# Two small columns, a table and small statistics move behind the work area, and every moving piece of a split product begins at 256 modulo 512 bytes

## The reference

```
u = rms_norm(x, g_mix[l]) * (1 + sc_a) + sh_a
proj = u @ w_in[l]
...
x = x + gt_a * (merged @ w_out[l])
u = rms_norm(x, g_ffn[l]) * (1 + sc_f) + sh_f
h = jax.nn.silu(u @ w_ffn_gate[l]) * (u @ w_ffn_up[l])
x = x + gt_f * (h @ w_ffn_down[l])
```

## Time and profile before

| | us |
|---|---|
| median of three runs | 2111.57 (2110.25 to 2115.39) |
| the profiled execution's own time | 2112.94 |
| its span, first to last instruction | 2111.1 |
| TensorE busy | 2038.4 (97%) |
| VectorE busy | 1624.9 (77%) |
| ScalarE busy | 1172.6 (56%) |
| mean granted TensorE clock | 0.992 |

### The profile page before, as it was taken

The page is one execution under the profiler, slowest core; times in us unless marked ns, Lnnn a source line. Parts: engine busy times, 40 slices in busy tenths (PEclk is TensorE's granted clock), DMA queues, the critical chain, the costliest instruction groups (busy, mean ns, idle before and its releaser), DMA issues.

```text
span 2111.1 us, 37052 instructions
## 1 busy us (share of the span) xinstructions
PE 2038.4 (97%) x13975; PEld 1849.3 (88%) x13975; DVE 1624.9 (77%) x2668; ACT 1172.6 (56%) x2116; POOL 148.0 (7%) x233
## 2 busy tenths in 40 slices
PE   6999999999999999998999999999999999999998
PEld 6988989999988989998876888888888888999997
DVE  7888879966688879978788789786889426657984
ACT  6757756645557756645637555352544226656762
POOL 0100000000000000004000210101102000000000
PEclk9999999999999999999999999999999999999999
DMA  9756547865666557876441334546644232243553
GB/s 359 277 205 207 173 159 249 277 233 167 224 231 208 171 170 236 293 250 199 153 165 48 124 120 150 192 148 224 222 143 140 90 100 91 91 151 132 187 183 117
DMA packets 106624, 383.03 MB, mean 181 GB/s; under 512 B 11504, under 2 KB 16128, under 8 KB 105184
## 3 DMA queue, kind: packets, MB, share of 16 engines
q1 hardware_dynamic: 77584, 280.21, 39.2%
q0 software_dynamic: 25792, 94.31, 13.5%
q10 hardware_dynamic: 3088, 6.29, 0.8%
HBM read 379.71 MB, written 1.05 MB: 180 GB/s over the span
## 4 chain that ended last, share of the span: by engine, by line
PE 80%; DVE 10%; DMA 3%; issue 3%; ACT 3%; POOL 0%; POOLq 0%; SPq 0%; DVEq 0%; ACTq 0%
PE ps L1100 20%; PE ps L1103 19%; PE ps L1104 19%; PE ps L1121 3%; PE ps L1125 3%; PE ps L1126 3%; DVE ring_l L2380 2%; DVE ada_junk L2403 2%; DMA work<-adas_in 2%; PE ps L1143 2%; PE ps L1147 1%; PE ps L1146 1%; PE ps L1673 1%; DMA ring<-tape_in 1%; PE ps L1338 1%
## 5 line engine op out<-in xcount | busy, mean ns | idle before, releaser
L1100 PE MATMUL ps<-part,ring_l 128*128 128x256 f32 (+1 forms) x3445 | 1040.9, 302 | 12.5 <-DVE ring_l L2380 8.1
L1103 PE MATMUL ps<-part,ring_r 128*128 128x256 f32 (+1 forms) x3445 | 1032.3, 300 | 0.0
L1104 PE MATMUL ps<-part,ring_r 128*128 128x256 f32 (+1 forms) x3445 | 1029.6, 299 | 0.0
L2380 DVE TENSOR_TENSOR ring_l<-ring,ring_r 128x1024 fp32r<-128x1024 f32 x514 | 626.5, 1232 | 151.0 <-ACT ring_r L1723 148.6
L1723 ACT ACTIVATE ring_r<-ring 128x1024 fp32r<-128x1024 f32 x514 | 533.8, 1056 | 362.9 <-DMA ring<-tape_in 264.9
L1100 PEld LDWEIGHTS ps<-part,ring_l 128*128 128x128 f32 x3445 | 649.3, 188 | 45.9 <-issue 7.6
L1104 PEld LDWEIGHTS ps<-part,ring_r 128*128 128x128 f32 x3445 | 649.4, 189 | 23.8
L1103 PEld LDWEIGHTS ps<-part,ring_r 128*128 128x128 f32 x3445 | 649.6, 189 | 22.1
L2403 DVE SCALAR_TENSOR_TENSOR ada_junk<-work 128x1024 bf16<-128x1024 f32 x272 | 333.9, 1228 | 49.2 <-DMA work<-adas_in 37.4
L1143 PE MATMUL ps<-part,ring_l 128*128 128x256 f32 (+1 forms) x400 | 125.2, 313 | 21.0 <-DVE part L2380 11.5
L1146 PE MATMUL ps<-part,ring_r 128*128 128x256 f32 (+1 forms) x400 | 121.6, 304 | 0.0
(11 more groups left out here) (287 smaller groups left out, 2110.9 us busy)
## 6 DMA issues: line engine op xcount, KB each, us to landing
ring<-tape_in SPq DMA_DIRECT2D x514, 512.0 KB, 3.4
work<-adas_in POOLq DMA_DIRECT2D x176, 512.0 KB, 4.7
work<-ada_first_in SPq DMA_DIRECT2D x8, 1024.0 KB, 17.2
work<-bias_in ACTq DMA_DIRECT2D x1, 2048.0 KB, 8.0
x<-x_t_in SPq DMA_DIRECT2D x1, 1024.0 KB, 7.6
work<-cond_in POOLq DMA_DIRECT2D x1, 1024.0 KB, 8.9
x<-ctx_in ACTq DMA_DIRECT2D x1, 1024.0 KB, 9.8
x<-dist_in ACTq DMA_DIRECT2D x1, 1024.0 KB, 6.1
```

The source lines that it names most:

```text
L1100: mm = pe.matmul(dst, lhsT=wl, rhs=mr, start=(k == 0), stop=False)
L1103: pe.matmul(dst, lhsT=wr, rhs=mr, start=False, stop=False)
L1104: mm = pe.matmul(dst, lhsT=wr, rhs=ml, start=False, stop=(k == len(moving) - 1))
L2380: return dve.tensor_tensor(dst, whole, rounded_part.bitcast(F32), ALU.subtract)
```

## The change

`fill` goes. `gs_mix`, `gs_ffn` and `misc` are laid behind `work`. Together these are 256 bytes, so `work` begins at 103,680, which is 256 modulo 512. The second stack's statistics (`na_max`, `na_sum`, `na_recip`, `ln_sum`, `ln_var`, `ln_rstd`) are laid in the last 108 floats of `work`, so `U2` begins at float 512. No instruction, wait or transfer is added, removed or put in another order. The start of the rings, and with it that of the weights, stays at 128 modulo 512.

```diff
-FILL = 8
...
-        gs_mix = sb("gs_mix", KD)
-        gs_ffn = sb("gs_ffn", KD)
...
-        misc = sb("misc", N_MISC)
...
-        fill = sb("fill", FILL)
...
         with nc.sbuf_tensor("work", [P, WORK + (ADA_SLOTS + N_COND) * D], F32) as work:
-            pass
+            with nc.sbuf_tensor("gs_mix", [P, KD], F32) as gs_mix, nc.sbuf_tensor("gs_ffn", [P, KD], F32) as gs_ffn, \
+                    nc.sbuf_tensor("misc", [P, N_MISC], F32) as misc:
+                pass
...
-        LN = place(3, 4)
-        ln_sum, ln_var, ln_rstd = (at(LN + 4 * n, 4) for n in range(3))
-        na_max, na_sum, na_recip = carve(2 * H, 2), carve(2 * H, 2), carve(2 * H, 2)
+        SMALL = WORK - 108
+        na_max, na_sum, na_recip = (at(SMALL + 4 * H * n, 2 * H, 2) for n in range(3))
+        ln_sum, ln_var, ln_rstd = (at(SMALL + 12 * H + 4 * n, 4) for n in range(3))
...
-        assert taken[0] <= WORK
+        assert taken[0] <= SMALL, taken[0]
```

More of the change, by code:

```diff
@@ L572, in two_blocks @@
         na_probs += [[at(SGU_B, T2), at(NA_BIAS, T2)], [carve(T2), at(NA_BIAS + H * T, T2)]]
-        assert taken[0] <= WORK
+        assert taken[0] <= SMALL, taken[0]
         na_keys = [at(SGU_W, 4, T), at(MIX_T, 4, T)]
         WIDE_SQ, WIDE_Y = BASE2, BASE2 + 12 * D
-        assert WIDE_Y + KD * T2 <= WORK and BASE2 + 9 * D < SGU
+        assert WIDE_Y + KD * T2 <= SMALL and BASE2 + 9 * D < SGU
         taken[0] = BASE2
@@ L591, in two_blocks @@
         wide_h = carve(2, T2)
-        assert taken[0] <= WORK, taken[0]
+        assert taken[0] <= SMALL, taken[0]
         taken[0] = BASE2
```

## The result

The changed kernel takes 2124.71 us (median of four runs, 2123.99 to 2124.97) against 2112.1 before (2110.25 to 2115.39). The ratio is 1.0056 with a 95% interval of 1.0038 to 1.0074: slower by 12.6 us. The forecast was 2071, with 0.20 for slower. What happened is rival 2, forecast at 2126.

The account below looks back on a forecast made before the run. TensorE, busy for 97% of the span, was taken as the bound, its pace hanging on operand starts. Gains of 28.1, 15.1 and 4.0 us, less 4.7 and 2.0, left 40.5 us: 2071 us, range 2038 to 2124.

Parts of the forecast that it names:

- rival 2: Moving pieces' starts: the pattern repeats at 256 bytes or less, so 256 is as 0; slower, 2126 us, chance 0.20.
- The start decides the possible paces and not the pace alone: TensorE's matmuls: products settle in one of several paces; one start, 448, showed both 117.7 and 113.4 ns.
- If closeness below the weights' start is what costs, 256 is among the good starts: Moving pieces: 256 lies furthest from 0, so it was given the trace's shortest step, 113.4 ns.
- The 28.1 us priced for the first stack: Gain for 5307 matmuls of 256 columns starting at 0, from 118.7 to 113.4 ns each.
- the 113.4 ns that I took for a start of 256: Step assumed for 256-column matmuls after the change, taken from the last output products at 448.
- the 15.1 us for the pieces at 448: Gain for 3500 of 4329 matmuls of 256 columns at 448, from 117.7 to 113.4 ns each.
- the 4.0 us for 512 columns: Gain for 1905 matmuls of 512 columns at 448, from 228.9 to 226.8 ns each.
- 10% for the chain's other links: Discount where the chain runs over VectorE, ScalarE or a transfer; 4.7 us off the main forecast's gain.
- The steps at 0 stay at 118.7 through long stretches: 256-column matmuls starting at 0: evidence that their pace differs from that at 448, against the start doing nothing.
- The stream's 233.3 at a start of 128: Streams of 512 columns, moving piece at 128: slower than 228.9 ns at 448, used as support for 256.
- Rival 1: TensorE's matmuls: the start does nothing or has small effects; time 2107 to 2113 us, chance 0.15.
- VectorE as the next limit: First feed-forward: TensorE would need 81.2 us while VectorE has 83.2 us of work, so 2.0 us are lost.

Follow-up runs that it names:

- all_192: Changed kernel with `par1_all` also laid behind `work`, so all moving pieces begin at 192 modulo 512: 2105.71 us, ratio 0.9967.
- all_440: `all_192` with `par` also behind `work` and every view of `work` shifted by 6 floats, so activations begin at 440: 2129.3 us, ratio 1.0086.
- ring192_work256: Changed kernel with 64 bytes ahead of the ring and `par1_all` behind a shorter `work`: weights at 192, activations at 256; 2106.68 us, ratio 0.9972.
- ring_r192_work256: Changed kernel with 64 bytes between the rings and `par1_all` behind a shorter `work`: `ring_l` at 128, `ring_r` at 192, activations at 256; 2101.65 us.
- base_only: Changed kernel with the statistics in front of `U2` again: first stack's gate and up pieces at 256, later ones at 192; 2109.22 us, ratio 0.9985.
- ring_r192_stack2_192: `ring_r192_work256` with the statistics in front again, so pieces from the down products on begin at 192: 2105.41 us, ratio 0.9975.

## Why the prediction was wrong

*What bounds the kernel, and that only addresses matter.* Right. Counts, waits and other engines are as before, and the loss lies in TensorE's steps.

*The start decides the possible paces and not the pace alone.* Right. At a distance of 64 a run of products settles at 113.3 or 117.8 ns; at 0 no 24 steps in a row have a mean below 118.2 ns in any of the three traces with all pieces there, and some run at 120.0. It might also explain why single times of a kernel at 64 scatter from 2098 to 2115 us (`all_192`, ten runs) and those of the changed kernel over 1 us (four runs). That is not shown: no kernel has several traces, and `all_440`, whose trace holds no short step, scatters from 2126 to 2140 us in five runs.

*The step that failed: "If closeness below the weights' start is what costs, 256 is among the good starts".* The idea that what matters lies between the moving piece and the weights beside it was right; `ring192_work256` shows it. I measured that distance around a circle of 512 bytes, for which I had no row. It repeats at 256 bytes, or at a part of that: 0, 128 below the weights' start, and 256, 128 above it, step alike, and so do 448 and 192, both 64 above it modulo 256. On that circle the change moves nothing for the first stack and takes everything else from the best place to one of the poor ones. The 28.1 us priced for the first stack came to nothing, since its step stayed at 118.7; the 113.4 ns that I took for a start of 256 occurs there in no stretch of 24 steps, the shortest of which has 118.2; the 15.1 us for the pieces at 448 had the wrong sign, as had the 4.0 us for 512 columns.

*Rival 2* priced the same facts as 7.7 us for 256 columns and 8.4 for 512. The traces have 6.5 and 8.3. Its one discount, 10% for the chain's other links, was small: 14.8 us became 12.1 in the span, 18% less, and no run shows that those links were the reason. It had 0.20 on the ground that no row told a period of 512 from one of 256 or 128. With two starts seen and the third unknown, that was the even question, and I answered it by the picture that I liked.

*Where rows were misread.* "The steps at 0 stay at 118.7 through long stretches" holds for the rows that I showed; other long stretches at 0 step at 120.0. Of the matmuls at 448 the trace has 725 short steps (at most 114.5 ns) where I took 800, but of the second layer's down products a quarter are short (139 of 581) and not most. The stream's 233.3 at a start of 128 was taken as a hint that a moving piece near the weights' place is slow. In fact streams step at 232 to 234 ns at every uniform distance, so they were no evidence about the activations.

*Rival 1 and the rule behind it.* The Trainium skill (TensorE: Matmul & The Clock Gate, section Step-by-step: what each phase is for) says that loading the next tile's weights takes no read bandwidth from the running matmul. If that were all, the place of the weights could not matter to the step. For float32r at full clock it does: 512-column activations at 256 step at 233.1 ns with weights at 128 (changed kernel) and at 228.9 with weights at 192 (`ring192_work256`). Whether bandwidth, or something else of the two reads, makes the difference no run shows.

*VectorE as the next limit* was not reached in any run. `ring_r192_work256` comes nearest: from 345 to 430 us it has 732 matmuls where the earlier trace rows have 718, VectorE busy for 83.23 us of the 85, and TensorE idle for 0.1 us.

## What to carry to other kernels

When TensorE runs float32r products back to back, read its step from the timeline, first start to last over the count; busy time hides it. Look for the start of the moving piece and of the weight tiles. In this kernel a moving piece 64 bytes behind the weights' start modulo 256 is worth 19 us of 2125 against one 128 behind; it is a place to try first elsewhere, and to measure. Before pricing an address by a distance, ask which rows fix its period: kernels that shift a single base by 64, 128 and 256 bytes answer it. The shift by 128 is the one that was not run here.

## What the runs showed of the hardware that was not expected

- The step depends on the distance between the moving piece and the weight tiles: 64 bytes apart modulo 256, 228.9 ns for 512 columns; 128 apart, 232.5 to 233.2, in three traces and with the ring in two places. The pattern repeats at 256 bytes; whether at 128 is open.
- 8 bytes beside the best place one shape is slow, and not the same one: 235.5 ns for 512 columns at 72, 120.0 for 256 at 56, while 512 columns at 56 keep 230.0. The Trainium skill (SBUF — State Buffer, section Door 1: The DMA port swizzle) tells of lines of 16 bytes in SBUF and of a penalty for each access that crosses to a new line. These two starts lie across such lines, and their kernels take longer than those at 48, 64 and 80, which do not. But 96, which begins a line, is as slow (119.9 and 233.3 ns), and lines of 16 explain none of the differences among 32, 48, 64, 80 and 96. So the runs do not show them to be the cause.
- At distance 64 long runs of equal matmuls keep one of two paces, 113.3 or 117.8 ns, with the same operands' starts modulo 512. What picks one is open; one kernel has both the earlier trace rows, and the same products had one in the kernel before (pieces at 448) and the other in `base_only` (at 192).
- With `ring_l` at distance 0 and `ring_r` at 64, 256 columns step at 115.9 ns, less than the mean at any uniform distance, while 512 columns step at 233.5. Why is open. Placing the 512-column pieces at a uniform 64 while the 256-column ones have the mixed distances was not tried, because both use the same rings.
- The kernel with the rings 64 bytes apart, 0.9964 (0.9948 to 0.9979), and `all_192`, 0.9967 (0.9949 to 0.9986), beat both the kernel before and the changed one; their intervals do not tell them apart. `ring192_work256`, `ring_r192_stack2_192` and `base_only` lie below the kernel before too.
